# Two-block transformer on one core: in block 2's sparse-attention heads, moving the multiply by the softmax coefficients to GpSimd and every second copy of turned probabilities to VectorE

## What is computed

```python
oc  = ... softmax over compressed keys ...
ps  = masked_softmax(ls, ds >= 0)                 # selected keys
os_ = einsum('bghqm,bgqmd->bghqd', ps, vsel)
pw  = masked_softmax(lw, (dw >= 0) & (dw < WINDOW) & (wpos >= 0))   # window
ow  = einsum('bghql,bgld->bghqd', pw, vw)
return gx[..., 0:1] * oc + gx[..., 1:2] * os_ + gx[..., 2:3] * ow
```

## Time and profile before

| | us |
|---|---|
| median of 3 runs | 2330.89 (2330.71 to 2331.95) |
| the profiled execution, its own time | 2330.6 |
| its span in the trace | 2328.8 |
| busy: PE / DVE / ACT / POOL | 2158.3 / 822.5 / 1051.8 / 1589.1 |

### The profile page before, as it was taken

The page is one execution under the profiler, slowest core; times in us unless marked ns, Lnnn a source line. Parts: engine busy times, 40 slices in busy tenths (PEclk is TensorE's granted clock), DMA queues, the critical chain, the costliest instruction groups (busy, mean ns, idle before and its releaser), DMA issues. The chain is left out here.

```text
span 2328.8 us, 33315 instructions
## 1 busy us (share of the span) xinstructions
PE 2158.3 (93%) x13112; PEld 1907.8 (82%) x13112; DVE 822.5 (35%) x1846; ACT 1051.8 (45%) x2020; POOL 1589.1 (68%) x1269
## 2 busy tenths in 40 slices
PE   6799999997769979999999999999999998999998
PEld 5688899786668879888768788999887687889996
DVE  3141455147451245517130136332151311363321
ACT  2254555454224445543444256544444532565443
POOL 5276688883238658889878332898898783328987
PEclk9799999997989989999999989999999999999999
DMA  6634345452004465444444620554454446305543
GB/s 224 135 120 170 109 158 169 163 206 97 1 35 148 144 191 181 164 180 172 154 145 147 205 107 27 176 185 173 183 181 145 145 147 203 108 33 175 186 174 130
DMA packets 217557, 343.16 MB, mean 147 GB/s; under 512 B 8473, under 2 KB 124281, under 8 KB 217275
## 3 DMA queue, kind: packets, MB, share of 16 engines
q1 hardware_dynamic: 206379, 331.60, 41.3%
q10 hardware_dynamic: 11024, 9.45, 2.0%
HBM read 336.83 MB, written 4.19 MB: 146 GB/s over the span
## 5 line engine op out<-in xcount | busy, mean ns | idle before, releaser
L1329 POOL TENSOR_TENSOR w_lo<-ring,w_hi 128x512 fp32r<-128x512 f32 x1184 | 1532.5, 1311 | 585.0 <-ACT w_hi L1424 533.1
L1424 ACT ACTIVATE w_hi<-ring 128x512 fp32r<-128x512 f32 x1184 | 739.0, 632 | 890.6 <-PE bank L697 350.5
L697 PE MATMUL bank<-x_hi,w_hi 128*128 128x256 f32 x2080 | 599.0, 288 | 47.7 <-POOL w_lo L1329 40.7
L700 PE MATMUL bank<-x_lo,w_hi 128*128 128x256 f32 x2080 | 594.3, 286 | 0.0
L701 PE MATMUL bank<-x_hi,w_lo 128*128 128x256 f32 x2080 | 594.0, 286 | 0.0
L697 PEld LDWEIGHTS bank<-x_hi,w_hi 128*128 128x128 f32 x2080 | 405.1, 195 | 54.8 <-issue 37.4
L700 PEld LDWEIGHTS bank<-x_lo,w_hi 128*128 128x128 f32 x2080 | 405.3, 195 | 0.2
L701 PEld LDWEIGHTS bank<-x_hi,w_lo 128*128 128x128 f32 x2080 | 404.9, 195 | 0.0
L722 PE MATMUL bank<-w_hi,x_hi 128*128 128x512 f32 x720 | 292.3, 406 | 13.7 <-POOL w_lo L1329 9.4
L725 PE MATMUL bank<-w_lo,x_hi 128*128 128x512 f32 x720 | 284.6, 395 | 0.0
L726 PE MATMUL bank<-w_hi,x_lo 128*128 128x512 f32 x720 | 284.3, 395 | 0.0
(11 more groups left out here) (311 smaller groups left out, 2404.2 us busy)
## 6 DMA issues: line engine op xcount, KB each, us to landing
ring<-in_w_in SPq DMA_DIRECT2D x72, 1024.0 KB, 6.8
ring<-in_ffn_w_up SPq DMA_DIRECT2D x44, 1024.0 KB, 7.6
ring<-in_w_ffn_in SPq DMA_DIRECT2D x44, 1024.0 KB, 7.3
ring<-in_ffn_w_down SPq DMA_DIRECT2D x20, 1024.0 KB, 6.0
ring<-in_w_ffn_out SPq DMA_DIRECT2D x20, 1024.0 KB, 5.9
ring<-in_xattn_wkv SPq DMA_DIRECT2D x16, 1024.0 KB, 6.1
ring<-in_w_o_ret SPq DMA_DIRECT2D x16, 1024.0 KB, 6.1
ring<-in_od_w_in SPq DMA_DIRECT2D x12, 1024.0 KB, 7.7
```

Source lines behind the costliest of these rows:

```text
L697: m = mm(out_, view(w_hi)[:, k, :], x_hi[:, 4 * kh + k, :], start=start, stop=False)
L700: mm(out_, view(w_hi)[:, k, :], x_lo[:, 4 * kh + k, :], start=False, stop=False)
L1329: tt(view(w_lo), src, view(w_hi), ALU.subtract).then_inc(w_lo_ready, 1)
L1424: return A(o, i_, ACT.Copy, **kw)
```

## The change

In block 2's heads (those with a gate), VectorE's `scale` stops behind the coefficients and raises a new semaphore, `coef_ready`. GpSimd gets a loop over the 32 heads of a layer, between `w_lo` of `mb1` and of `onsa0`: it waits for `coef_ready`, multiplies `E` (128x128 and 128x256) and raises `p_ready`. The copies to `PT` of the odd heads go from ScalarE to VectorE, where they stand in step s for head s-3, behind `scale` of head s-1 and ahead of `store_mixed`. Block 1's heads and the cross-attention stay as they are.

```diff
@@ gpsimd
-                remainders(f"{L}qn0", f"{L}qn1", f"{L}mb0", f"{L}mb1", f"{L}onsa0", f"{L}onsa1", f"{L}out0", f"{L}out1")
+                remainders(f"{L}qn0", f"{L}qn1", f"{L}mb0", f"{L}mb1")
+                for hd in nsa_heads(i):
+                    r = hd.at % 4
+                    pool.wait_ge(coef_ready, hd.kw["n_exp"] - A_HEADS + 1)
+                    for t, lo, hi in ((0, 0, P), (1, P, 384)):
+                        m = ts(E[:, r, lo:hi], E[:, r, lo:hi], coef[:, r, t:t + 1], None, ALU.mult)
+                    m.then_inc(p_ready, 1)
+                remainders(f"{L}onsa0", f"{L}onsa1", f"{L}out0", f"{L}out1")
@@ scalar
             def probabilities(hd):
+                if hd.kw.get("gate") and hd.at % 2:
+                    return
                 n = 512 if hd.kw["cross"] else 384
@@ vector
                         scale(hs[step - 1])
+                    if 3 <= step < n + 3 and hs[step - 3].kw.get("gate") and hs[step - 3].at % 2:
+                        probabilities(hs[step - 3])
                     if 4 <= step and step - 4 < n:
                         out(hs[step - 4])
+
+            def probabilities(hd):
+                b = B.uses[(hd.key, "T")][0]
+                B.wait_full(dve, (hd.key, "T"))
+                nc.vector.tensor_copy(PT[:, hd.at % 2, 0:384], bank[b][:, 0:384]).then_inc(empty[b], 1)
@@ vector, scale
                 if kw.get("gate"):
-                    tt(coef[:, r, :], coef[:, r, :], kw["gates"], ALU.mult)
-                    drain()
+                    tt(coef[:, r, :], coef[:, r, :], kw["gates"], ALU.mult).then_inc(coef_ready, 1)
+                    return
                 for t, lo, hi in parts:
                     m = ts(E[:, r, lo:hi], E[:, r, lo:hi], coef[:, r, t:t + 1], None, ALU.mult)
                 m.then_inc(p_ready, 1)
```

More of the change, by code:

```diff
@@ L403, in build @@
         exp_ready = sem("exp_ready")
+        coef_ready = sem("coef_ready")
         p_ready = sem("p_ready")
```

## The result

The changed kernel is slower: 2336.35 us, median of 20 runs (2331.53 to 2342.85), against 2332.34 us for the kernel before in its 20 runs (2330.03 to 2335.6). The ratio is 1.0018, with a 95% interval of 1.0011 to 1.0025, so about 4.2 us, between 2.6 and 5.8. It lies outside the range that was forecast (2328.0 to 2334.2) and on its slow side, though the difference of 0.18% is still what the prediction called "the same" (within 0.2%). Of the 6.3 us between the forecast of 2330.1 and the 2336.35 measured, 1.5 us are no effect of the change: the forecast was added to a median of 3 runs, 2330.89, and the median of before in 20 runs is 2332.34. The profiled execution took 2337.48 us.

The account below looks back on a forecast made before the run. TensorE was taken to bound block 2's heads. A layer gains 0.19 us at the start and 0.57 at the end and loses 0.39 between: 0.7 us in two layers, forecast 2330.1 us, range 2328.0 to 2334.2.

Parts of the forecast that it names:

- the same: Whole time: a difference from the kernel before of under 0.2% (4.7 us); chance 0.89.
- What bounds the kernel: Block 2's heads: TensorE is busy throughout, VectorE 84%, so the 29 us taken from VectorE is hidden.
- GpSimd's pair: GpSimd's two multiplications of E for each head: bounded by 0.76 and 1.32 us, taken at 0.85 us.
- Nothing in between reaches 1.87 us: Any pair time between the bounds stays under TensorE's pace of 1.87 us a head, so GpSimd keeps up.
- hand-off: From the end of GpSimd's last multiplication to TensorE's start: about 0.25 us, against 0.05 us behind VectorE.
- The start of the heads: First turns of a layer's block 2 heads: a gain of 0.19 us, or a loss of 0.45 at 1.32 us a pair.
- rival 1: GpSimd's pair slow but under the pace (1.1 to 1.8 us), or VectorE's copies late: 2331 to 2335 us; chance 0.20.
- The odd copy behind the store: VectorE's copy to PT queued behind a store of eight heads: 0.13 us late, three times a layer.
- The end: Last heads up to onsa0: wait for w_lo gone, head 29's values 0.33 us late; gain of 0.57 us a layer.
- Rival 3: VectorE's small multiplication of the coefficients waits out GpSimd's instruction, up to 0.79 us each time: 2337 us; chance 0.05.

Follow-up runs that it names:

- pool_imm: The changed kernel, but GpSimd multiplies by a constant 1/128 instead of the coefficients; 2331.95 us in its only run.
- pool_tt: The changed kernel, but GpSimd multiplies tensor by tensor with the coefficient's column broadcast; 2331.12 us, ratio 0.9996 to the kernel before.
- copy_only: The kernel before, but VectorE takes the odd heads' copies to PT and still does the multiplications; 2343.96 us, ratio 1.0054 to before.
- last_copy: The kernel before, with only head 31's copy to PT moved to VectorE; 2330.55 us, ratio 1.0 to before.
- slow_start: The kernel before, with two extra VectorE multiplications by one ahead of head 0's multiplications, making the first turn late; 2335.64 us, ratio 1.0021 to before.

## Why the prediction was wrong

**What bounds the kernel.** Right. TensorE is full inside the heads in the changed kernel too, and the 29 us taken from VectorE bought nothing.

**GpSimd's pair: the step that failed.** It was bounded by 0.76 and 1.32 us and taken at 0.85; it is 1.53, outside both bounds. The upper bound rested on the assumption that a one-input instruction can't cost more than a two-input one, and the lower slope on memsets, which read nothing. `pool_imm` and `pool_tt` show it the wrong way round: 2.5 ns an element with one input, 1.7 with two. Here the trace also contradicts the Trainium skill (GPSIMD Engine Reference, section Engine selection: one input at roughly line rate): the pair takes 1.53 us on GpSimd and 0.55 on VectorE. Its advice to keep elementwise work off GpSimd would have given the right sign. "Nothing in between reaches 1.87 us" held; the margin was smaller than thought. A second term erred the other way: the hand-off was taken at 0.25 us from one wait of `onsa0`, and measured 0.05 at every turn that waited for GpSimd. Pair and hand-off together were forecast at 1.10 us and are 1.60.

**The start of the heads.** Forecast as a gain of 0.19 us, and as a loss of 0.45 at 1.32 us a pair; measured a loss of 0.85 at 1.53. The chain was right, its duration was not, and the 0.45 does not follow from it: head 1's pair would end at 1382.20 + 2 x 1.32 = 1384.84, its turn would start at 1385.09 and `values`, 0.33 us behind the turn as in the forecast (1384.58 - 1384.25), at 1385.42: a loss of 0.65. With that, rival 1 at 1.32 us should have been priced 0.2 us a layer higher.

**The odd copy behind the store.** Forecast 0.13 us three times a layer. The place was right: behind all six stores the weight load starts 0.05 us after the copy's end. But TensorE's matmuls stood still for it only once, 0.19 us in two layers. VectorE's copy takes 0.55 us, as estimated. Three of the five waits of `copy_only` show the mechanism at full size.

**The end.** Forecast a gain of 0.57 us with head 29's copy late. `last_copy` shows that 0.97 us are to be had. In the change the last two turns waited 0.25 and 0.28 us for GpSimd instead, and of the gain at the end nothing is left: the start's loss of 0.85 us and the layer's of 0.96 differ by 0.1.

**The rivals.** Rival 1 came true in its mechanism, priced at +0.15 us a layer for 1.32 us and +2 for 1.7; measured +0.96 and +1.30 at 1.53, between the two. Rival 3, mutual exclusion, did not come: VectorE's small multiplication takes 162 ns in the median and 258 ns at most. Nor was that for want of meetings, as the prediction had argued: with the longer pair 34 of the 64 small multiplications overlap one of GpSimd's in time, and 13 lie wholly inside a single one of 0.6 or 0.9 us, 10 of them at 0.16 us and three at 0.19 to 0.26.

**What no step contained.** A longer wait of TensorE at the start of the heads can cost more than itself, since the granted clock then falls in some of the executions. 5 of 10 layers at about 1.6 us are 1.6 us an execution; with the 2.3 us of waits that makes 3.9 us, and about 4.2 were measured (2.6 to 5.8). `slow_start` shows that the late turn alone, with nothing on GpSimd, can bring it about. That it accounts for just the missing part rests on ten layers and is an estimate. Against it stands `copy_only`: its whole time is 12.7 us over before (9.1 to 16.1, 5 runs) and its heads only 8.9, without a longer first wait and without the lower clock in its heads. Its trace shows nothing longer behind them, and those 3.8 us are unexplained. Why the lower clock strikes one layer and not its fellow stays open too.

## What to carry to other kernels

Where one engine is full, work taken from its neighbours is worth only what it changes at the edges of the stage, so move the last item (one copy gave 1 us a layer in the heads, too little to be seen in the whole time) and leave the others where they are. A slower engine in a pipeline's chain is paid for at the first and last turns even when its throughput suffices. And bound an operation that the trace doesn't have by measuring it, since one input is not always cheaper than two.

## What the runs showed of the hardware

On GpSimd, fp32 in SBUF: a multiplication by a per-partition factor took 606 ns for 128 elements and 926 for 256, by a constant 531 and 851, and by a broadcast tensor column 399 and 612. The form with the broadcast is the fastest of the three. From the end of GpSimd's instruction to the start of TensorE's transpose that waited for it passed 0.05 us, as behind VectorE.

VectorE's multiplication of 128x2 elements, with both inputs in SBUF, ran in 0.16 us wholly inside a GpSimd multiplication in 10 of 13 cases of the changed kernel's profile, and in at most 0.26 in the other three.

The granted clock of TensorE fell to its lower level in the first microseconds of the heads only in kernels in which the first turn waited 1.5 us, in 6 of 16 layers with 1.4 us or more and in none of 12 with 0.9 us or less. It cost 1.5 to 1.7 us each time.
